# Network one's turns and attentions in two stages without inner barriers, and query tiles in the order 128, 256, 512, 384 keys

## The chip, the cores and the metric

The program runs on one core of a Trainium2 chip, in one launch. The metric is the device time of the whole program in microseconds (us). The engines are TensorE (PE, matrix products), VectorE (DVE), ScalarE (ACT), GpSimd (POOL) and SyncE (SP), which issues the weight loads.

## The reference

Two networks of two layers each, on 512 tokens of width 1024, in float32. Network one, per layer: rmsnorm, one wide projection, and three mixers side by side, then an output projection and a squared-relu feed-forward. The mixers are

- `mla_attention`: 8 heads, queries and keys of 96 (64 plain, 32 with rope), values of 64, causal softmax;
- `dsa_attention`: 4 heads of 64 with one shared key and value head; a query sees only the 128 keys that an index score ranks highest (`lax.top_k`), found here as a mask;
- `retention`: 4 heads of 64, `(q k^T * decay) v`, written in the kernel without chunks, then a group norm times `silu(gate)`.

Network two, per layer: a gated delta rule, a block-compressed attention with 6 heads, two further softmax attentions of 6 heads each over the same tokens, a stick-breaking attention, and a gated feed-forward with a convolution. Of it the change touches only the two softmax attentions ("nsa", 12 heads in one call).

## The kernel before

Tokens are tiled by 128, so a head has four query tiles; causal tile t has (t+1) x 128 keys. A stage (`Core.stage`, L151) is one block of instruction streams, one per engine, written out by hand; at its end all engines meet in a barrier (its instructions are at L168). With `goes_on=True` a stage ends without a barrier and the next one's instructions follow in the same streams; then the waits must be written out. `stay_busy` (L178) issues eight transposes without use on PE at a stage's end.

Network one's mixers are five stages in a row in each layer:

1. "mlaT" (`transpose_tiles`, L463): 16 jobs, the turns of 8 key heads and then 8 query heads. A job is four 128-column transposes into PSUM bank i % 8; even jobs are kept (copied to SBUF) by ACT, odd ones by DVE.
2. "mla" (`softmax_attention`, L2570): 32 units, a unit being a head and a query tile. For unit i PE issues the scores of i (L2611, float32, two passes), then the turn of the probabilities of i-2 (L2625), then the values of i-4 (L2635). DVE adds the causal mask (L2653), takes the maximum (L2654); ACT takes the exponential with the row sum (L2686) and then copies the turned probabilities of unit i-2 (L2697). The turn of unit u waits for the exponential of u and the copy of u-2. After a head's last tile DVE divides (L2667, L2669). GpSimd ropes the other mixers' columns meanwhile.
3. "mixT" (`transpose_tiles`): seven jobs, the shared "dsa" key (split in a high and a low part, by ACT and then DVE, L535), two of its queries, two of the retention's queries, two of its keys. ACT first does the Silu of the gate (L4086) and two casts.
4. "ret" (`retention`, L2700): PE's dots (L2720) for pairs of heads in banks 0 to 5, the product with the decay on DVE (L2751), the outputs (L2730) in banks 6 and 7, squares and copies on ACT. DVE also finishes the search of the largest index scores (L1126, L1128, L1130), makes the first query's low part (L459) and sums the squares (L2761). GpSimd multiplies the gate (L2766).
5. "dsa" (`softmax_attention`): 16 units; scores as two single-pass products and the mask as a third (L2614), so DVE adds no mask. GpSimd does the retention's group norm.

In the attentions the units of a head run in the order of 128, 256, 384 and 512 keys. "nsa" of network two is the same function with a `guest`, the tail of the compressed attention, whose steps are placed by unit number; it already follows its turns without a barrier.

Of the kernel before, what the change touches and what calls it, by code (L numbers as in the profile page):

```python
# [462 lines left out]
def transpose_tiles(c, name, jobs, also_pool=None, also_act=None, first_dve=None, wait_source=None, by_dve=None):  # L463
# [15 lines left out]
    with c.stage(name, "turned", "act_kept", "dve_kept", "made") as (block, turned, act_kept, dve_kept, made):  # L479
# [4 lines left out]

        @block.tensor
        def _(pe):
            def wait_kept(i):
                if i in by_dve:
                    pe.wait_ge(dve_kept, by_dve.index(i) + 1)
                else:  # L490
                    pe.wait_ge(act_kept, by_act.index(i) + 1)

            for i, (src, m, dst, scale) in enumerate(jobs):
                if i >= 8:
                    wait_kept(i - 8)
# [12 lines left out]
            if len(jobs) >= 8:  # L508
                wait_kept(len(jobs) - 8)
            c.stay_busy(pe, len(jobs) % 8, 8)  # L510

        @block.scalar
        def _(act):
            if also_act is not None:
                also_act(act)
            for i, (src, m, dst, scale) in enumerate(jobs):
                if i in by_act:
                    act.wait_ge(turned, i + 1)
                    if i in split:
# [4 lines left out]
                    ins.then_inc(act_kept, 1)  # L524

        @block.vector
        def _(dve):
            if first_dve is not None:
                first_dve(dve, made)
            for i, (src, m, dst, scale) in enumerate(jobs):  # L530
# [6 lines left out]
                if i in by_dve:  # L537
# [3 lines left out]
                    ins.then_inc(dve_kept, 1)  # L541

# [590 lines left out]
SEARCH_EARLY = 15  # L1133

# [1435 lines left out]
def softmax_attention(c, name, heads, meanwhile=None, beside=None, ready=None, guest=None):  # L2570
# [7 lines left out]
    units = [(h, t) for h in range(len(heads)) for t in range(TT)]  # L2578
    U = len(units)
    with ExitStack() as ctx:  # L2580
# [8 lines left out]
        with c.stage(name, "scores", "maxed", "probs", "turned", "probsT", "outs", "kept", "step", "pool_step",  # L2589
# [8 lines left out]
            def _(pe):  # L2598
                for i in range(U + 4):
                    if i < U:  # L2600
# [6 lines left out]
                        if t == 0 and ready is not None:  # L2607
                            ready(pe, beside_done, h)
# [9 lines left out]
                    if 0 <= u < U:  # L2618
# [3 lines left out]
                        elif guest is not None:  # L2622
                            guest.wait_turn(pe)
                        for j in range(units[u][1] + 1):
# [4 lines left out]
                    if 0 <= u < U:  # L2629
                        h, t = units[u]  # L2630
                        pe.wait_ge(probsT, u + 1)
                        if t == 0 and h >= 2:
                            pe.wait_ge(kept, h - 1)
                        for j in range(t + 1):
# [9 lines left out]
            def _(dve):  # L2644
                step = Steps(dve, step_sem)
                for i in range(U + 5):
# [14 lines left out]
                    if 0 <= u < U and units[u][1] == TT - 1:  # L2661
# [14 lines left out]
            def _(act):  # L2676
                for i in range(U + 3):
                    if i < U:
# [5 lines left out]
                        if t == 0 and h >= 4:  # L2684
# [15 lines left out]
def retention(c, name, qT, kT, v, decay, out, gate, g_ret, var, beside, queries):  # L2700
# [5 lines left out]
    with ExitStack() as ctx:  # L2706
        sb = lambda n, s: ctx.enter_context(c.tile(name + n, s, F32))
        inner = sb("inner", [P, RET_H, TT, SEQ])
        sq, warm = sb("sq", [P, RET_H, TT, HD]), sb("warm", [P, 1])
        with c.stage(name, "dots", "inners", "outs", "kept", "step", "squares", "q_his", "q_los") as (  # L2710
                block, dots, inners, outs, kept, step_sem, squares, q_his, q_los):
            @block.tensor
            def _(pe):
                def dot_pairs(k):
                    pair, j = k // TT, k % TT
                    if k >= 3:
                        pe.wait_ge(inners, 2 * (k - 2))
                    for b in range(2):
                        r = slice(HD * b, HD * (b + 1))
                        nc.tensor.matmul(c.ps[:, 2 * (k % 3) + b, 0:SEQ - j * P],  # L2720
                                         kT[r, pair, j * P:(j + 1) * P], qT[r, pair, j * P:SEQ],
                                         start=True, stop=True).then_inc(dots, 1)

                def out_of(h):
                    pe.wait_ge(inners, 2 * TT * (h // 2 + 1))
                    if h >= 2:
                        pe.wait_ge(kept, h - 1)
                    for t in range(TT):
                        for j in range(t + 1):
                            ins = nc.tensor.matmul(  # L2730
                                c.ps[:, 6 + h % 2, t * HD:(t + 1) * HD],
                                inner[:, h, j, (t - j) * P:(t - j + 1) * P],
                                v[:, j, h * HD:(h + 1) * HD], start=(j == 0), stop=(j == t))
                    ins.then_inc(outs, 1)

                for k in range(6):
                    dot_pairs(k)
                out_of(0)
                for k in range(6, 2 * TT):
                    dot_pairs(k)  # L2740
                for h in range(1, RET_H):
                    out_of(h)
                c.stay_busy(pe, 0, 8)

            @block.vector
            def _(dve):
                step = Steps(dve, step_sem)
                for i in range(RET_H * TT):
                    pair, j, b = i // (2 * TT), i // 2 % TT, i % 2
                    dve.wait_ge(dots, i + 1)  # L2750
                    nc.vector.tensor_tensor(inner[:, 2 * pair + b, j, 0:SEQ - j * P],  # L2751
# [1655 lines left out]
```

## Time and profile before

| | us |
|---|---|
| median of 3 runs | 3170.96 (3170.54 to 3171.04) |
| the profiled execution | 3171.36 |
| its span, first to last instruction | 3169.3 |

| engine | busy us | share |
|---|---|---|
| PE | 3076.0 | 97% |
| DVE | 1810.4 | 57% |
| ACT | 1288.5 | 41% |
| POOL | 402.4 | 13% |

The shares are means over stages that have different limits. The ends of PE's instructions are modelled, and one can begin while the one before it still runs, so PE's stalls are read from starts. In the rows a time is from the span's start.

### The profile page before, as it was taken

What the parts mean: (1) busy time and instruction counts of PE and PEld (TensorE: products, weight loads), DVE (VectorE), ACT (ScalarE), POOL (GpSimd) and SP (SyncE); (2) the same over time, 40 slices, a digit from 0 to 9 for tenths busy, and PEclk for the clock granted to TensorE, in tenths of its full rate; (3) what the DMA queues carried; (4) which work ended last, traced back from release to release, by engine and by line L of the source; (5) the groups of instructions that cost most, each with busy time, mean ns of one, the idle gap of its engine ahead of it and who ended that gap; (6) DMA issues with size and microseconds to landing.
All of it is one profiled execution on the core that took longest, in us unless ns stands there. A gap on an engine that the chain in (4) does not pass through costs nothing. (4 is left out here: it accounts for less than half of the span.)

```text
span 3169.3 us, 48184 instructions
## 1 busy us (share of the span) xinstructions
PE 3076.0 (97%) x19220; PEld 2618.1 (83%) x19220; DVE 1810.4 (57%) x3220; ACT 1288.5 (41%) x2673; POOL 402.4 (13%) x398
## 2 busy tenths in 40 slices
PE   8999999999999999999999999999999999999997
PEld 6878888888878888888888888888888878888886
DVE  4876443435965434357566467474575665574655
ACT  4445432334354423244374343232643643332325
POOL 1031000001031000002213302010003034010010
PEclk9999999999999999999999999999999999999999
DMA  4110222222201322322100122223222000222221
GB/s 176 57 54 28 94 93 98 102 84 89 83 2 54 107 93 94 125 74 100 67 1 2 42 80 100 90 93 117 81 101 80 1 2 22 94 97 95 91 95 63
DMA packets 37293, 239.38 MB, mean 76 GB/s; under 512 B 4432, under 2 KB 5200, under 8 KB 15056
## 3 DMA queue, kind: packets, MB, share of 16 engines
q1 hardware_dynamic: 36080, 233.58, 21.6%
q8 instruction: 154, 2.52, 0.3%
q10 hardware_dynamic: 992, 2.73, 0.3%
q14 instruction: 67, 0.55, 0.1%
HBM read 234.19 MB, written 2.10 MB: 75 GB/s over the span
## 5 line engine op out<-in xcount | busy, mean ns | idle before, releaser
L278 PE MATMUL ps<-b_hl,bff_whl 128*128 128x512 f32 (+1 forms) x840 | 313.6, 373 | 0.0
L279 PE MATMUL ps<-b_hl,bff_whl 128*128 128x512 f32 (+1 forms) x840 | 313.2, 373 | 0.0
L280 PE MATMUL ps<-b_hl,bff_whl 128*128 128x512 f32 (+1 forms) x840 | 313.2, 373 | 0.0
L261 DVE SCALAR_TENSOR_TENSOR bff_whl<-ring,b_cols,bff_whl 128x512 fp32r<-128x512 f32 (+3 forms) x288 | 194.7, 737 | 186.4 <-ACT bff_whl L248 186.1
L248 ACT ACTIVATE bff_whl<-ring,b_cols 128x512 fp32r<-128x512 f32 (+3 forms) x288 | 173.4, 674 | 168.7 <-PE ps L280 168.7
L278 PE MATMUL ps<-a_hl,aff_whl 128*128 128x512 f32 (+1 forms) x648 | 238.9, 369 | 0.0
L279 PE MATMUL ps<-a_hl,aff_whl 128*128 128x512 f32 (+1 forms) x648 | 238.5, 368 | 0.0
L280 PE MATMUL ps<-a_hl,aff_whl 128*128 128x512 f32 (+1 forms) x648 | 238.5, 368 | 0.0
L258 DVE TENSOR_TENSOR aff_whl<-ring,aff_whl 128x512 fp32r<-128x512 f32 x160 | 99.8, 686 | 216.6 <-ACT aff_whl L246 216.5
L278 PE MATMUL ps<-aff_whl,a_hl 128*128 128x512 f32 (+5 forms) x544 | 204.9, 377 | 4.5 <-DVE a_hl L680 2.2
L279 PE MATMUL ps<-aff_whl,a_hl 128*128 128x512 f32 (+5 forms) x544 | 202.3, 372 | 0.0
L280 PE MATMUL ps<-aff_whl,a_hl 128*128 128x512 f32 (+5 forms) x544 | 202.3, 372 | 0.0
L278 PE MATMUL ps<-aff_whl,a_u 128*128 128x512 f32 x512 | 199.5, 390 | 0.0
L261 DVE SCALAR_TENSOR_TENSOR aff_whl<-ring,a_gains,aff_whl 128x512 fp32r<-128x512 f32 (+3 forms) x192 | 131.9, 748 | 117.9 <-ACT aff_whl L248 117.5
L280 PE MATMUL ps<-aff_whl,a_u 128*128 128x512 f32 x512 | 199.2, 389 | 0.0
L279 PE MATMUL ps<-aff_whl,a_u 128*128 128x512 f32 x512 | 199.2, 389 | 0.0
L246 ACT CAST aff_whl<-ring 128x512 fp32r<-128x512 f32 x160 | 87.5, 621 | 268.4 <-PE ps L280 263.6
L248 ACT ACTIVATE aff_whl<-ring,a_gains 128x512 fp32r<-128x512 f32 (+3 forms) x192 | 120.0, 697 | 174.9 <-PE ps L280 174.9
L280 PEld LDWEIGHTS ps<-b_hl,bff_whl 128*128 128x128 f32 x840 | 158.2, 188 | 27.9
L279 PEld LDWEIGHTS ps<-b_hl,bff_whl 128*128 128x128 f32 x840 | 158.2, 188 | 27.7
L278 PEld LDWEIGHTS ps<-b_hl,bff_whl 128*128 128x128 f32 x840 | 158.2, 188 | 27.6
L258 DVE TENSOR_TENSOR bff_whl<-ring,bff_whl 128x512 fp32r<-128x512 f32 x128 | 84.6, 720 | 141.7 <-ACT bff_whl L246 141.6
(512 smaller groups left out, 7240.7 us busy)
## 6 DMA issues: line engine op xcount, KB each, us to landing
ring<-in_a_w_ff SPq DMA_DIRECT2D x64, 1024.0 KB, 4.7
ring<-in_b_w_up SPq DMA_DIRECT2D x32, 1024.0 KB, 4.8
ring<-in_a_w_in SPq DMA_DIRECT2D x16, 1024.0 KB, 4.8
ring<-in_b_w_down SPq DMA_DIRECT2D x16, 1024.0 KB, 4.8
ring<-in_b_w_in_att SPq DMA_DIRECT2D x12, 1024.0 KB, 4.7
ring<-in_b_w_up SPq DMA_DIRECT2D x16, 768.0 KB, 4.1
ring<-in_b_w_in_conv SPq DMA_DIRECT2D x12, 768.0 KB, 4.2
ring<-in_a_w_out SPq DMA_DIRECT2D x8, 1024.0 KB, 4.9
```

Source lines behind the costliest of these rows:

```text
L246: self.c.nc.scalar.copy(self.part(j, 0, k), src[:, k, :]).then_inc(self.hi_made, 1)
L248: self.c.nc.scalar.activation(self.part(j, 0, k), src[:, k, :], ACT.Copy, scale=g[:, row + k:row + k + 1]).then_inc(self.hi_made, 1)
L258: self.c.nc.vector.tensor_tensor(self.part(j, 1, k), src[:, k, :], self.part(j, 0, k).bitcast(F32), ALU.subtract).then_inc(self.lo_made, 1)
L261: self.c.nc.vector.scalar_tensor_tensor(out=self.part(j, 1, k), in0=src[:, k, :], scalar=g[:, row + k:row + k + 1], in1=self.part(j, 0, k) ...
L278: nc.tensor.matmul(bank, sh, mh, start=start, stop=False)
L279: nc.tensor.matmul(bank, sh, ml, start=False, stop=False)
L280: return nc.tensor.matmul(bank, sl, mh, start=False, stop=stop)
```

## The change

"mlaT" and "mla" become one stage, and "mixT", "ret" and "dsa" another: `transpose_tiles` and `retention` are called with `goes_on=True`, issue no transposes without use, and return the waits that the next part needs. The jobs of "mlaT" alternate, key and query of a head after each other. Those of "mixT" begin with the retention's, and the Silu and the two casts move from ACT's first place to its last. The retention's tiles are allocated with the others of the stage. In `softmax_attention` the tiles of a head run in the order (0, 1, 3, 2), for all three attentions of both networks.

```diff
+TILE_ORDER = (0, 1, 3, 2)
-    units = [(h, t) for h in range(len(heads)) for t in range(TT)]
+    units = [(h, t) for h in range(len(heads)) for t in TILE_ORDER]
...
+class TurnsInFront:
+    def __init__(self, kept):
+        self.kept = kept
+    def wait_score(self, pe, i):
+        h, t = i // TT, i % TT
+        if t == 0 and h < MLA_H:
+            self.kept(pe, 2 * h)
+            self.kept(pe, 2 * h + 1)
+        if i < 4:
+            self.kept(pe, 8 + i)
+    def wait_turn(self, pe, u):
+        self.kept(pe, 12 + u)
+    def wait_out(self, pe, h):
+        self.kept(pe, 14 + h)
+class RetentionInFront:
+    def wait_score(self, pe, i):
+        if i == 0:
+            self.turned(pe, 4)
+            self.turned(pe, 5)
+            pe.wait_ge(self.cleared, 1)
+            pe.wait_ge(self.q_los, 1)
+    def wait_turn(self, pe, u):
+        pe.wait_ge(self.outs_kept, u + 1)
+    def wait_out(self, pe, h):
+        pe.wait_ge(self.outs_kept, RET_H - 1 + h)
+    def wait_norm(self, pool):
+        pool.wait_ge(self.gated, 1)
+        pool.wait_ge(self.outs_kept, RET_H)
+        pool.wait_ge(self.sums, RET_H)
...
 transpose_tiles:
-            if len(jobs) >= 8:
-                wait_kept(len(jobs) - 8)
-            c.stay_busy(pe, len(jobs) % 8, 8)
+            if not goes_on:
+                if len(jobs) >= 8:
+                    kept(pe, len(jobs) - 8)
+                c.stay_busy(pe, len(jobs) % 8, 8)
...
 retention, PE:
                 if k >= 3:
                     pe.wait_ge(inners, 2 * (k - 2))
+                else:
+                    kept_turn(pe, 2 * k)
+                    kept_turn(pe, 2 * k + 1)
...
                 if h >= 2:
                     pe.wait_ge(kept, h - 1)
+                elif h == 0:
+                    kept_turn(pe, 6)
...
-            c.stay_busy(pe, 0, 8)
 retention, POOL and ACT:
+            pool.wait_ge(made, 1)
+            pool.wait_ge(acted, 1)
...
+                kept_turn(act, 5)
+                kept_turn(act, 6)
...
 first_layer:
-            jobs = [(lambda t, h=h: kcat[:, t, h, :], MLA_QK, kT[0:MLA_QK, h, :], 1.0) for h in range(MLA_H)]
-            jobs += [(lambda t, h=h: q4[:, t, h, :], MLA_QK, qT[0:MLA_QK, h, :], mla_scale) for h in range(MLA_H)]
-            transpose_tiles(c, "mlaT", jobs)
+            jobs = []
+            for h in range(MLA_H):
+                jobs += [(lambda t, h=h: kcat[:, t, h, :], MLA_QK, kT[0:MLA_QK, h, :], 1.0),
+                         (lambda t, h=h: q4[:, t, h, :], MLA_QK, qT[0:MLA_QK, h, :], mla_scale)]
+            kept, all_turned, _, _ = transpose_tiles(c, "mlaT", jobs, goes_on=True)
...
-            jobs = [(lambda t: (proj[:, t, A_AK:A_AK + DSA_D],) * 2, P, SplitKeys(kbhi[:], kblo), 1.0)]
+            jobs = []
+            for i in range(2):
+                jobs += [(tile_of(A_RQ + i * P), P, rqT[:, i, :], RET_D ** -0.5),
+                         (tile_of(A_RK + i * P), P, rkT[:, i, :], 1.0)]
+            jobs += [(lambda t: (proj[:, t, A_AK:A_AK + DSA_D],) * 2, P, SplitKeys(kbhi[:], kblo), 1.0)]
             jobs += [(tile_of(A_AQ + i * P), P, qbT[:, i, :], DSA_D ** -0.5) for i in range(2)]
-            jobs += [(tile_of(A_RQ + i * P), P, rqT[:, i, :], RET_D ** -0.5) for i in range(2)]
-            jobs += [(tile_of(A_RK + i * P), P, rkT[:, i, :], 1.0) for i in range(2)]
...
-            transpose_tiles(c, "mixT", jobs, clear, gates)
+            kept, _, made, acted = transpose_tiles(c, "mixT", jobs, clear, last_act=gates, goes_on=True)
...
+            def query_low(dve, done, i):
+                if i in (0, 4, 8):
+                    dve.wait_ge(front.q_his, i // 4 + 2)
+                    queries.low(dve, done, i // 4 + 1)
```

## Rows read from the trace of the kernel before

**Rows 1.** Page, busy us, share of the span and instructions of each engine

```profile
PE 3076.0 (97%) x19220; PEld 2618.1 (83%) x19220; DVE 1810.4 (57%) x3220; ACT 1288.5 (41%) x2673; POOL 402.4 (13%) x398
```

**Rows 2.** Stretches: length, busy of PE, PEld, DVE, ACT, POOL; granted clock; DMA

```profile
201.60:250.97 49.37, 46.96 (x312) 36.60 (x312) 32.23 (x83) 29.17 (x96) 24.73 (x18) 1.00 0.00 1
...
257.80:261.90 4.10, 4.06 (x16) 2.66 (x16) 2.35 (x5) 3.84 (x6) 2.78 (x4) 0.58 0.01 2
...
941.32:944.72 3.40, 2.70 (x16) 1.52 (x16) 2.23 (x5) 3.31 (x6) 2.78 (x4) 1.00 0.00 0
```

**Rows 3.** Timeline, "mlaT" to "mla": start, us, engine, line, count [idle before <-releaser]

```profile
200.32 1.04 PE L180 MATMUL ps<-const_a 128*128 128x128 f32 x8
200.52 0.69 DVE L540 TENSOR_SCALAR a_qT<-ps 96x512 f32<-96x512 f32 x1 [0.19 <-PE ps L504]
...
202.15 0.30 DVE L2653 TENSOR_TENSOR ps<-ps,const_a 128x128 f32<-128x128 f32 x1 [0.94 <-PE ps L2611]
...
206.79 0.41 PE L2625 MATMUL ps<-const_a,mlap 128*128 128x128 f32 x2 [0.38 <-ACT mlapT L2697]
```

**Rows 4.** Timeline, one head of "mla" and the next one's 512 score

```profile
226.49 0.56 DVE L2654 TENSOR_REDUCE mlanegmax<-ps 128x1 f32<-128x384 f32 x1
226.69 1.08 PE L2611 MATMUL ps<-a_kT,a_qT 96*128 96x512 f32 x2
227.08 0.58 ACT L2686 ACTIVATE mlap<-ps,mlanegmax 128x384 f32<-128x384 f32 x1 [0.68 <-DVE mlanegmax L2654]
...
227.60 0.39 PE L2625 MATMUL ps<-const_a,mlap 128*128 128x128 f32 x2
...
228.13 0.69 DVE L2654 TENSOR_REDUCE mlanegmax<-ps 128x1 f32<-128x512 f32 x1
...
228.86 0.69 ACT L2686 ACTIVATE mlap<-ps,mlanegmax 128x512 f32<-128x512 f32 x1 [0.95 <-DVE mlanegmax L2654]
...
229.44 0.65 PE L2611 MATMUL ps<-a_kT,a_qT 96*128 96x256 f32 x2
...
230.04 0.63 PE L2625 MATMUL ps<-const_a,mlap 128*128 128x128 f32 x4
...
232.33 1.08 PE L2611 MATMUL ps<-a_kT,a_qT 96*128 96x512 f32 x2
```

**Rows 5.** Timeline, the end of "mla"

```profile
246.98 0.63 PE L2625 MATMUL ps<-const_a,mlap 128*128 128x128 f32 x4 [0.72 <-ACT mlapT L2697]
...
248.09 0.59 ACT L2697 COPY mlapT<-ps 128x512 f32<-128x512 f32 x1 [0.88 <-PE ps L2635]
```

**Rows 6.** Timeline, "mixT", "ret" and the start of "dsa"; last row: layer two

```profile
251.01 1.09 PE L506 MATMUL ps<-const_a,a_proj 128*64 128x128 f32 x16 [0.30 <-PEq L168]
...
252.04 2.84 PE L504 MATMUL ps<-const_a,a_proj 128*128 128x128 f32 x24
...
256.84 0.68 DVE L540 TENSOR_SCALAR a_rkT<-ps 128x512 f32<-128x512 f32 x1
...
257.84 5.84 PE L2720 MATMUL ps<-a_rqT,a_rkT 64*128 64x512 f32 x24 [2.09 <-PEq L168]
...
259.55 3.36 DVE L2751 TENSOR_TENSOR retinner<-ps,const_a 128x512 f32<-128x512 f32 x8 [2.03 <-PE ps L2720]
...
263.61 2.44 PE L2730 MATMUL ps<-a_proj,retinner 128*128 128x64 f32 x20
...
266.71 1.15 DVE L2751 TENSOR_TENSOR retinner<-ps,const_a 128x256 f32<-128x256 f32 x4 [1.44 <-PE ps L2720]
...
273.42 1.40 DVE L2761 TENSOR_REDUCE a_var<-retsq 128x4 f32<-128x256 f32 x4
...
275.68 0.29 DVE L2654 TENSOR_REDUCE dsanegmax<-ps 128x1 f32<-128x128 f32 x1 [0.86 <-PE ps L2614]
...
942.49 0.69 DVE L2751 TENSOR_TENSOR retinner<-ps,const_a 128x512 f32<-128x512 f32 x1 [1.45 <-PE ps L2720]
```

**Rows 7.** Waits of PE in "nsa", 1568.75 to 1642.6: us in total, times, longest

```profile
PE ps L2625 <- ACT nsapT L2697: 4.1, 5, 2.3
```

More of the change, by code:

```diff
@@ L478, in transpose_tiles @@
     split = [i for i, job in enumerate(jobs) if isinstance(job[2], SplitKeys)]
-    with c.stage(name, "turned", "act_kept", "dve_kept", "made") as (block, turned, act_kept, dve_kept, made):
+    with c.stage(name, "turned", "act_kept", "dve_kept", "made", "acted", goes_on=goes_on) as (
+            block, turned, act_kept, dve_kept, made, acted):
         if also_pool is not None:
@@ L524, in _ @@
                     ins.then_inc(act_kept, 1)
+            if last_act is not None:
+                last_act(act, acted)
         @block.vector
@@ L2606, in _ @@
                             guest.wait_score(pe, i)
-                        if t == 0 and ready is not None:
+                        if front is not None:
+                            front.wait_score(pe, i)
+                        if i % TT == 0 and ready is not None:
                             ready(pe, beside_done, h)
@@ L2660, in _ @@
                     u = i - 5
-                    if 0 <= u < U and units[u][1] == TT - 1:
+                    if 0 <= u < U and u % TT == TT - 1:
                         h = units[u][0]
@@ L2697, in _, with retention @@
                         nc.scalar.copy(pT[:, u % 2, 0:nk], c.ps[:, 4 + u % 2, 0:nk]).then_inc(probsT, 1)
-def retention(c, name, qT, kT, v, decay, out, gate, g_ret, var, beside, queries):
+def retention(c, name, qT, kT, v, decay, out, gate, g_ret, var, beside, queries,
+              tiles, kept_turn, made, acted):
     nc = c.nc
[L2706 to L2742, printed above, removed]
-                c.stay_busy(pe, 0, 8)
[L2745 to L2751, printed above, removed]
-                                            c.ps[:, 2 * (i // 2 % 3) + b, 0:SEQ - j * P],
-                                            decay[:, 2 * pair + b, 0:SEQ - j * P], ALU.mult).then_inc(inners, 1)
-                for i in range(9):
-                    beside(dve, step, i)
-                if queries is not None:
-                    dve.wait_ge(q_his, 1)
-                    queries.low(dve, q_los, 0)
-                for h in range(RET_H):
-                    dve.wait_ge(squares, h + 1)
-                    nc.vector.tensor_reduce(var[:, :, h], sq[:, h], AX.X, ALU.add)
-            @block.gpsimd
-            def _(pool):
-                for t in range(TT):
-                    nc.gpsimd.tensor_tensor(gate[:, t], gate[:, t], g_ret, ALU.mult)
-            @block.scalar
-            def _(act):
-                nc.scalar.activation(warm[:], decay[:, 0, 0:1], ACT.Exp)
-                if queries is not None:
-                    for f in range(queries.n):
-                        queries.high(act, f).then_inc(q_his, 1)
-                for h in range(RET_H):
-                    act.wait_ge(outs, h + 1)
-                    o = c.ps[:, 6 + h % 2, 0:TT * HD].rearrange("p (t d) -> p t d", t=TT)
-                    nc.scalar.activation(sq[:, h], o, ACT.Square).then_inc(squares, 1)
-                    nc.scalar.copy(out[:, :, h, :], o).then_inc(kept, 1)
@@ L2781, in group_norm @@
+    return kept, q_his, q_los, sums, gated
 def group_norm(nc, pool, step, out, gate, sums, half):
```

122 lines of the change are left out of this document (101 added, 21 removed).

## The prediction

> **What bounds the kernel now.** I read the engines' shares first: TensorE (PE) is busy 97% of the span [rows 1]; its busy ends are modelled, so the share hides short stalls. So I read start against start in the timeline. The stages that the change touches were found with the table by stretch; it shows the attention stage "mla" with PE working in 46.96 of 49.37 us, VectorE (DVE) in 32.23, ScalarE (ACT) in 29.17 [rows 2]. Inside it PE's instructions follow one another without a hole: one head (four query tiles) takes 232.33 - 226.69 = 5.64 us of PE start to start [rows 4]. The time that isn't PE's own work lies at the seams of stages (fill, barrier, drain), and once a head. The retention stage is different: there PE waits for DVE.
>
> The change acts in both layers of network one (joins, order) and both of network two (order alone). Layer two of network one repeats layer one 683.52 us later (the stretches 257.80 and 941.32 begin the same stage).
>
> **Join of the turns and "mla".** Before, the last transposes end where PE's eight filler transposes begin, 200.32; they and the barrier hold the first mask addition on DVE until 202.15 [rows 3]. Afterwards PE can issue the first score at 200.32, but DVE still has the keep of turn 15 to finish, 200.52 + 0.69 = 201.21 [rows 3]. So DVE, and with it the first exponential and turn, starts at about 201.24, 0.91 us earlier: not the 1.33 by which PE is freed, since DVE is late next. The turn at 206.79 waited a further 0.38 us for a copy [rows 3]. That wait goes: with 512 keys third, the fourth unit's scores are shorter and its chain starts earlier, while the third's is 0.24 us longer (maximum and exponential of 512 for 384, [rows 4]); I take 0.3. Added waits: two semaphores a head on PE, both signalled one or more turns earlier, behind them only PE's own queue; I cost them at nothing since PE is bound by the array here; if each cost 0.05 us uncovered, 8 heads x 2 x 2 layers would be 1.6 us. Other ends of this term: 0 if DVE's queue eats it, 1.6 if the third unit costs nothing. Taken: 1.2 a layer, **2.4 us**. GpSimd's ropes start after the last turn, about 1 us earlier, and nobody waits for them.
>
> **Order of the tiles, steady state.** PE does score(i), turn(i-2), values(i-4). The turn of a 512 tile waits for maximum, exponential and one copy. Before, from PE's end of issue of the 512 scores (227.60) to the turn (230.04) passed 2.44 us, after which PE waits for ACT [rows 4]. The PE work between is about 2.32: a 512 score takes 227.60 - 226.69 = 0.91 in two passes, one of 256 should take 0.48, and 230.04 - 229.44 is 0.60 [rows 4]. So a stall of some 0.12 a head is hidden where no idle shows. In the new order the turn of 512 comes after a 384 score and 384 values more: PE work between about 2.8, needed 2.44, no stall. The tight one is then 384: the PE work from its score to its turn is 2.32 less a block of values twice over (values of 384 for 512, -0.22) plus a transpose (+0.11), about 2.2; needed is 2.44 less the difference in maximum (0.69 to 0.56) and exponential (0.69 to 0.58), 2.20 [rows 4]. The slack is nil, within 0.1 either way. I take the gain of 0.12 for the seven heads after the first: 0.85 a layer, **1.7 us**; bounds -1.6 (a new stall of 0.1 each) to +1.9. ACT pairs exponential and copy more evenly, which buys nothing while PE is the bound. In "dsa" and network two's "nsa" the mask is a product on PE and DVE has one step less, so there is no such stall to win in their steady state, and 0.3 us more slack for the 384 turn.
>
> **Order, drain.** At the end of "mla" the turn of the last 512 tile waits 0.72 us, and its copy at 248.09 holds the last values [rows 5]. With 384 last, maximum, exponential and copy are 0.13, 0.11 and 0.10 shorter, and the copy of 512 lies before, under PE's values. Of the 0.72 about 0.1 goes. PE's last values then stand behind a 0.59 copy that ACT, idle for 0.88, could begin only when PE had finished another tile's values [rows 5]; I estimate 0.4 of it uncovered, and nearly all of that goes. I take 0.5 a stage; six stages ("mla", "dsa", "nsa", two layers each): **3.0 us**, bounds 1 and 4.
>
> **"nsa", the rest.** Five turns wait 4.1 us for a copy, one of them 2.3 [rows 7]; the largest is in the fill, where the third unit is now 512 and some 0.25 us later, and the periodic ones wait for a copy that is now of 384 (0.1 shorter) with PE arriving slightly later. +0.5 less 0.25 a layer: **0.5 us**, bounds -2 and +3, since DVE's and ACT's guest work is placed by unit number and meets other sizes.
>
> **Second join: turns, retention, "dsa".** This is the largest term. Before: PE ends the seven jobs at 251.01 + 1.03 + 24 x 0.11 = 254.7 [rows 6]. ACT first did Silu and two casts, so DVE's five keeps end at 256.84 + 0.68 = 257.52, and only after the barrier come the dots (257.84) and the first product with the decay, 259.55 [rows 6]. Afterwards: the retention's four jobs first, Silu last. PE turns rq, rk pairs by 251.01 + 16 x 0.11 = 252.8, the shared key by 253.8; ACT casts it by about 254.6; DVE then has three passes of 0.69 (two subtractions, one keep) to 256.75. Dots 0 and 1 are issued at 254.7, behind the transposes, so the first decay product starts at about 256.8: 2.75 earlier than 259.55, and 2.15 earlier than 942.49 in layer two (258.97 in layer one's time) [rows 6].
>
> DVE then runs its eight products in the same 3.36; the next dots wait for DVE's products as before, then PE does 20 value passes in 2.44 (before they began at 263.61), and the products before 266.71 come out at about 264.05, 2.66 earlier in layer one and 2.0 in layer two [rows 6]. From there to the end of the variance sums (273.42 + 1.40 = 274.82) DVE's chain is unchanged, so it ends 272.16. The third barrier goes: the first maximum of "dsa" came at 275.68, 0.86 after that sum [rows 6]; PE issues those scores behind its last retention values, and DVE takes the maximum at once. Together 2.66 + 0.86 = 3.5 and 2.0 + 0.86 = 2.9, 6.4 us. Silu and the second table load, now late on ACT, end near 260, before ACT's next customer (retention's first output, about 263.3); if ACT were late there, PE would wait at the third output, not before. GpSimd's gate product moves after Silu, and its norm starts when the sums are there; the stage ends 20 us later, so both are hidden.
>
> What PE's clock takes off: PE stood idle 2.09 us before 257.84 [rows 6], and in 257.80 to 261.90 the granted clock was 0.58, that is mostly 1.2 GHz, while the same dots in layer two (941.32 to 944.72) ran at 1.00, 2.4 GHz [rows 2]. After the change the filler transposes are gone and PE waits for DVE's products in three gaps of 0.6 to 0.8 us between 256.4 and 259.3. If the clock falls there, dots 4 and 5 and the 20 value passes (2.44) run at half speed: up to 1.5 us a layer is lost. One layer in two: -0.8. Bounds 3 and 7; taken **5.6 us**.
>
> The Trainium skill, "TensorE: Matmul & The Clock Gate", "What's actually happening", says that an array that has been too little busy is passed only half its clock and gets the rest back after a stretch of activity. By that rule the lost filler speaks against the change, and both layers would lose; that is part of rival B.
>
> **Sum.** 2.4 + 1.7 + 3.0 + 0.5 + 5.6 = 13.2 us. The profiled execution took 3171.36 (span 3169.3), 0.4 over the median of 3170.96. 3171.36 - 13.2 = 3158.2, as a median 3157.8.
>
> **Rivals.**
> (A) The joins give, the order doesn't: PE is the bound in all three attentions, the 0.12 isn't a stall and the drains are as long. For it: no idle shows in steady state; against it: the 0.72 before the last turn. Then 0.9 x 2 + 5.6 = 7.4, 3163.6.
> (B) The retention chain keeps its end: the dots wait for DVE twice more, PE's clock falls in both layers, and only about half of the 6.4 arrives. For it: the 0.58 of rows 2; against it: DVE's own passes are unchanged in length. 13.2 - 2.4 = 10.8, 3160.2.
> (C) Slower: in the new order the turn of the 384 tile waits for the copy of the 256 tile behind its exponential. Its slack in "mla" is nil by the numbers above; there are 12 heads in each layer of network one and 12 in each of network two, 48 in all. Without the order's 5.2 the joins give 8.0, so it decides from 8.0 / 48 = 0.17 us a head; at 0.35 it costs 16.8 and the time is 3179.8. Against it: in 32 of those heads DVE has no mask addition and the slack is about 0.3.
> (D) The change doesn't do what it says: the first stage's scores still wait, since DVE's keeps and the last turn end together; the seams give only barrier times (0.3 us of PE at each of six). Then 1.8 + 3.0, 3166.2.
> (E) More than forecast: "nsa" gains at each periodic stall and no clock falls: 3153.
>
> **Chances.** Forecast (3155.5 to 3160) 0.55, A 0.13, B 0.13, C 0.04, D 0.04, E 0.11. A measurement of this kernel can tell about 0.2%, 6.3 us. Above 3164.6 lie D and the upper part of A: no change 0.09; slower than 3177.3 only C, 0.04; faster 0.87. The range takes in E, B and most of A: 3152.5 to 3164.
>
> **What would show it.** Right: no filler transposes between turns and scores; the first mask addition of "mla" right behind DVE's last keep; a head in "mla" of 5.50 to 5.55 us instead of 5.64; the first decay product about 5.8 us after the second join starts; the first "dsa" maximum right behind the variance sums; a shorter wait before the last turn in all six attentions. Wrong: PE idle before the 384 turns in every head; granted clock below 1 from about 6 us after the join's start in both layers; decay products that begin where they did; a longer fill in "nsa".

## The result, and the profile after

| | us | runs |
|---|---|---|
| before | 3171.0 (3170.54 to 3172.64) | 4 |
| after | 3152.25 (3149.84 to 3155.82) | 4 |
| after / before | 0.9942 [0.9931, 0.9954] | |

The change makes the kernel faster by 18.7 us, where 13.2 were forecast. The median lies under the forecast's 3155.5 to 3160 and 0.25 us under the lower end of the whole range, 3152.5 to 3164. The profiled execution of the changed kernel took 3151.79, its span is 3150.0, that is 19.3 less than before. How much of that is the change's own is settled further below, where the same kernel is run again.

The page after, engines (busy us, share, instructions), against [rows 1]. PE's work is 14.6 us less in sum, part of it the 48 transposes without use that are gone and part the clock.

```profile
PE 3061.4 (97%) x19172; PEld 2605.8 (83%) x19172; DVE 1808.8 (57%) x3220; ACT 1292.5 (41%) x2673; POOL 402.1 (13%) x398
```

The stages, from PE's first instruction of one to that of the next, in the table by stretch (columns as in [rows 2]). Kernel before: "mlaT" and "mla"; "mixT" to "dsa" of layer one and of layer two; "nsa" with its turns; the delta rule and what follows up to the second "nsa"; the last 599 us; and one stretch inside the delta rule of the first network-two layer.

```profile
193.32:251.01 57.69, 55.00 (x384) 44.43 (x385) 37.72 (x91) 33.96 (x105) 24.77 (x19) 1.00 0.00 1
251.01:299.13 48.12, 44.57 (x344) 39.04 (x345) 29.87 (x65) 25.69 (x70) 11.50 (x10) 0.96 0.01 2
...
934.57:982.03 47.46, 43.20 (x345) 37.91 (x346) 29.80 (x65) 25.66 (x71) 11.47 (x10) 1.00 0.00 1
1544.70:1642.69 97.99, 90.91 (x804) 86.74 (x805) 59.80 (x146) 59.82 (x173) 5.03 (x5) 0.97 0.07 23
...
1685.78:2428.97 743.19, 733.21 (x5076) 631.27 (x5077) 448.48 (x702) 274.77 (x517) 126.68 (x124) 1.00 0.24 81
...
2570.04:3169.28 599.24, 573.20 (x4296) 491.49 (x4296) 347.72 (x540) 210.57 (x402) 97.41 (x103) 0.99 0.22 74
...
1715.70:1719.10 3.40, 3.04 (x56) 3.04 (x58) 0.00 (x0) 0.91 (x3) 0.31 (x1) 0.50 0.00 0
```

The same stages of the kernel after:

```profile
192.50:247.89 55.39, 52.79 (x376) 43.55 (x377) 37.93 (x91) 34.08 (x104) 24.78 (x19) 1.00 0.00 1
247.89:291.81 43.92, 41.20 (x328) 35.91 (x329) 28.50 (x65) 26.46 (x70) 11.49 (x10) 1.00 0.01 1
924.89:968.81 43.92, 41.19 (x328) 35.91 (x329) 28.49 (x65) 26.46 (x70) 11.50 (x10) 1.00 0.01 1
1531.50:1628.25 96.75, 90.61 (x804) 86.26 (x805) 59.95 (x146) 60.87 (x173) 5.02 (x5) 0.96 0.07 23
1671.33:2412.44 741.11, 730.90 (x5076) 628.79 (x5077) 448.77 (x702) 274.78 (x517) 126.70 (x124) 1.00 0.24 81
...
2552.19:3150.00 597.81, 572.26 (x4296) 490.53 (x4296) 347.62 (x540) 210.68 (x402) 97.34 (x103) 0.99 0.22 74
```

Per stage: "mla" 57.69 to 55.39, -2.30; layer two shows the same (57.69 to 55.37). "mixT" to "dsa" 48.12 to 43.92, -4.20, and 47.46 to 43.92, -3.54; the two layers differed before by 0.66 because the granted clock fell in layer one [rows 2], and don't after. "nsa" 97.99 to 96.75, -1.24 (layer two -1.36). The feed-forwards are unchanged. The last two pairs are code that the change doesn't touch: -2.08 and -1.43. There the clock differs: the stretch from 1715.70 ran at half clock before (0.50) and its counterpart after didn't. That isn't all of it, as the second profile of the same kernel shows further below. The sum is 2.30 + 2.32 + 4.20 + 3.54 + 1.24 + 1.36 + 3.51 = 18.5, and with 0.8 in the first 193 us, untouched too, 19.3.

The first join in the timeline after, against [rows 3]. The stage starts at 192.50 (before 193.32).

```profile
199.70 0.69 DVE L548 TENSOR_SCALAR a_qT<-ps 96x512 f32<-96x512 f32 x1 [0.19 <-PE ps L509]
...
200.31 0.28 DVE L2717 TENSOR_TENSOR ps<-ps,const_a 128x128 f32<-128x128 f32 x1
...
203.62 0.63 PE L2687 MATMUL ps<-const_a,mlap 128*128 128x128 f32 x4 [0.73 <-ACT mlapT L2761]
```

DVE goes from the last keep to the first mask addition without idle time, 7.81 us after the stage's start; before it was 202.15 - 193.32 = 8.83. But the turn of the 512 tile, now the third unit's, waits 0.73 us in the fill. Before, two turns shared that wait: the fourth unit's, of 512 keys, waited 0.38 [rows 3], and the third's, of 384 keys, 0.29:

```profile
205.24 0.52 PE L2625 MATMUL ps<-const_a,mlap 128*128 128x128 f32 x3 [0.29 <-ACT mlapT L2697]
```

One head of "mla" after, and its end, against [rows 4, 5]:

```profile
224.77 0.86 PE L2671 MATMUL ps<-a_kT,a_qT 96*128 96x384 f32 x2
...
227.19 0.65 PE L2671 MATMUL ps<-a_kT,a_qT 96*128 96x256 f32 x2
...
227.68 0.51 PE L2687 MATMUL ps<-const_a,mlap 128*128 128x128 f32 x3
...
230.29 0.86 PE L2671 MATMUL ps<-a_kT,a_qT 96*128 96x384 f32 x2
...
244.24 0.52 PE L2687 MATMUL ps<-const_a,mlap 128*128 128x128 f32 x3 [0.59 <-ACT mlapT L2761]
244.59 2.12 PE L2699 MATMUL ps<-a_proj,mlapT 128*128 128x64 f32 x18
245.24 0.48 ACT L2761 COPY mlapT<-ps 128x384 f32<-128x384 f32 x1 [0.66 <-PE ps L2699]
```

A head takes 230.29 - 224.77 = 5.52 us instead of 5.64. The difference lies in one place. From the start of the 256 tile's scores to the start of the turn behind them it is 227.68 - 227.19 = 0.49 us; before it was 230.04 - 229.44 = 0.60 [rows 4], where that turn was the 512 tile's. This is the hidden stall of the prediction. At the end the last turn waits 0.59 instead of 0.72, and the 18 value products (4, 8 and 6, for 256, 512 and 384 keys) run through without a break while ACT copies.

The second join, against [rows 6]:

```profile
247.89 1.28 PE L509 MATMUL ps<-const_a,a_proj 128*128 128x128 f32 x10 [0.30 <-PEq L168]
...
253.64 3.28 DVE L2818 TENSOR_TENSOR a_ret_inner<-ps,const_a 128x512 f32<-128x512 f32 x8
...
253.76 0.70 PE L2786 MATMUL ps<-a_rqT,a_rkT 64*128 64x256 f32 x4 [0.18 <-DVE a_qbT L548]
...
254.99 0.49 PE L2786 MATMUL ps<-a_rqT,a_rkT 64*128 64x128 f32 x4 [0.53 <-DVE a_ret_inner L2818]
...
255.91 1.77 PE L2786 MATMUL ps<-a_rqT,a_rkT 64*128 64x512 f32 x8 [0.44 <-DVE a_ret_inner L2818]
...
267.43 1.40 DVE L2828 TENSOR_REDUCE a_var<-a_ret_sq 128x4 f32<-128x256 f32 x4
...
268.75 0.28 DVE L2718 TENSOR_REDUCE dsanegmax<-ps 128x1 f32<-128x128 f32 x1
```

The decay products start 5.75 us after the stage's start (before 259.55 - 251.01 = 8.54), the variance sums 19.54 after it (before 22.41), and the first maximum of "dsa" follows them without idle time, 20.86 after (before 24.67).

### The profile page after: what moved, and what is told of

The parts are those of the page before. It is cut to its first block and busy times, and to the rows that moved or that the text cites. A ratio compares the mean times of both kernels' runs of the same rounds, so it can differ in the third digit from the quotient of the medians.

```text
span 3150.0 us, 48082 instructions
## 1 busy us (share of the span) xinstructions
PE 3061.4 (97%) x19172; PEld 2605.8 (83%) x19172; DVE 1808.8 (57%) x3220; ACT 1292.5 (41%) x2673; POOL 402.1 (13%) x398
```

## The experiments

All kernels were timed beside the kernel before on the same chip; a ratio is to that one. The kernel before spread over 3165.65 to 3173.37 in 21 runs of the first group, so the ratios alone don't separate effects of 1 us. The lengths of the stages that the change touches do: in network one they agree to 0.1 us between kernels that are equal there, in "nsa" to 0.2 where it runs equally long at half clock.

### e1: the joins alone

```diff
 (after)
-TILE_ORDER = (0, 1, 3, 2)
+TILE_ORDER = (0, 1, 2, 3)
```

> The changed kernel with the tiles of a head back in the order 128, 256, 384, 512; both joins stay. Theory (the order gives in all three attentions): a head of mla takes 5.64 us of PE start to start again (5.52 in the changed kernel), the last turn of mla waits about 0.88 again, mlaT to the end of mla is about 56.5 us (55.4 changed, 57.7 before), mixT to the end of dsa about 43.8 (43.45 changed), nsa with its turns 97.7 (96.4 changed); total 3157 to 3160. Rival A (the joins give, the order does not): mla's stretch stays at 55.4 and nsa's at 96.4, total like the changed kernel's 3152. Theory on the rest: about 3.5 us of the changed kernel's gain are three stretches of half clock in network two, outside the change, that its profile no longer shows; whether they are in this run decides 3.5 us of its time either way.

3161.35 in 6 runs, 0.9971 [0.996, 0.9983]. "mla", "mixT" to "dsa", and "nsa" of this kernel:

```profile
192.97:249.58 56.61, 53.89 (x376) 43.53 (x377) 37.58 (x91) 33.91 (x104) 24.77 (x19) 1.00 0.00 1
249.58:293.73 44.15, 41.47 (x329) 36.02 (x329) 28.60 (x65) 26.22 (x70) 11.49 (x10) 1.00 0.01 1
1534.91:1631.56 96.65, 89.51 (x805) 85.12 (x805) 59.72 (x147) 59.96 (x173) 5.01 (x5) 0.98 0.07 23
```

The first join is worth 57.69 - 56.61 = 1.08 a layer, the second 47.46 - 44.15 = 3.31. Two heads take 236.54 - 225.25 = 11.29 us (starts of the 512 scores), 5.64 each, as before. The last turn waits 0.72, as before; the 0.88 of the expectation is the wait of ACT's copy [rows 5]. "nsa" is 96.65 and not 97.7 because only 3.4 us of it ran at half clock in this layer; in the other, with 6.8, it is 97.97.

### e2: the order alone

```diff
 (before)
+TILE_ORDER = (0, 1, 3, 2)
-    units = [(h, t) for h in range(len(heads)) for t in range(TT)]
+    units = [(h, t) for h in range(len(heads)) for t in TILE_ORDER]
...
-                        if t == 0 and ready is not None:
+                        if i % TT == 0 and ready is not None:
...
```

The last lines stand for four like ones: a head's first and last tile are now told by the unit's number.

> The kernel before with the new order of tiles alone, no join. Theory: a head of mla 5.52 us, its last turn waits about 0.75 instead of 0.88, nsa with its turns 96.4 instead of 97.7, dsa 0.4 shorter; the gains per layer about 1.2 (mla), 0.4 (dsa), 1.3 (nsa), together 5.8 us: 3165, less up to 3.5 if stretches of half clock in network two go. Rival (384 turns stall, or order neutral): heads of 5.64 or more and 3171.

3164.52 in 10 runs, 0.9981 [0.9972, 0.999]. "mla", "mixT" to "dsa", and "nsa":

```profile
193.41:249.86 56.45, 53.81 (x385) 44.44 (x385) 37.98 (x91) 34.12 (x105) 24.77 (x19) 1.00 0.00 1
249.86:296.97 47.11, 42.63 (x344) 37.92 (x345) 29.80 (x65) 25.92 (x70) 11.51 (x10) 1.00 0.01 2
1540.94:1637.59 96.65, 90.46 (x805) 86.51 (x805) 59.94 (x147) 60.86 (x173) 5.02 (x5) 0.96 0.07 23
```

The order is worth 1.24 in "mla", 0.35 in "dsa", 1.34 in "nsa" (97.99 to 96.65, both with 6.8 us at half clock). With the joins' 1.08 the 2.32 of "mla" comes out, and 3.31 + 0.35 is 3.66 where the whole change shows 3.54: the parts add up.

### e3, e4: what in the second join pays, Silu's place, the jobs' order or the barriers

```diff
 (e3, from after: ACT does Silu and the casts before its keeps again)
-            if also_act is not None:
-                also_act(act)
+            if last_act is not None:
+                last_act(act, acted)
...
-            if last_act is not None:
-                last_act(act, acted)
 (e4, from before, with the tile order: the jobs' new order in "mlaT" and "mixT",
  also_act behind ACT's keeps; barriers and transposes without use stay)
```

> The changed kernel with the gate's Silu and the two casts again ahead of ACT's keeps in the joined stage; joins and job order stay. Theory (the second join pays because the retention's keeps come first on ACT and DVE): Silu with its table load holds ACT until about 2.7 us after the stage's start, so the keep of the first retention query comes at +2.8 instead of +0.7, the dots at +3.8 as before the edit, but the key's cast and DVE's three passes behind it later by about 1 us: first decay product at about +6.8 instead of +5.8, total +1 to +2 us. Rival (only the barriers count, ACT's order does not): +5.8 and no difference.

> The kernel before with the new order of tiles, the new order of the turn jobs and Silu last, but with all barriers and filler transposes kept. Theory: the jobs' order buys nothing behind a barrier beyond the end of DVE's keeps (from +6.55 to about +5.8 us of the stage), so retention's first product comes at about +7.8 (layer one; +8.6 before, +5.8 changed) and mixT to the end of dsa takes about 46 (47.6 and 47.0 before, 43.45 changed); total 3163 less up to 3.5 for half clock elsewhere. Rival: the job order is the whole gain of the second join and the barriers are free: +5.8 or so and 43.5.

Silu first: 3154.97 in 4 runs, 0.9949 [0.9934, 0.9964]; the stage is 44.49 in both layers against 43.92, so its place is worth 0.57 a layer. The first product came 6.32 us after the stage's start, where 6.8 were expected and the changed kernel has 5.75. The jobs' order and Silu's new place without the joins: 3166.42 in 10 runs, 0.9988 [0.9979, 0.9998], no better than the tile order alone, and the stage got longer where about 46 us were expected. Its two layers:

```profile
248.93:297.86 48.93, 43.98 (x344) 38.54 (x345) 30.02 (x65) 26.34 (x70) 11.49 (x10) 0.97 0.01 2
932.04:981.82 49.78, 45.30 (x344) 39.48 (x345) 30.06 (x65) 26.36 (x70) 11.51 (x10) 0.93 0.00 1
```

And its timeline where the retention's dots begin:

```profile
256.60 3.96 PE L2721 MATMUL ps<-a_rqT,a_rkT 64*128 64x512 f32 x16 [2.81 <-PEq L168]
...
258.68 2.27 DVE L2752 TENSOR_TENSOR retinner<-ps,const_a 128x512 f32<-128x512 f32 x4 [4.03 <-PE ps L2721]
```

With a barrier behind it, Silu at the end is what all engines wait for: PE idles 2.81 us, then has half its clock, and the products start 9.75 us after the stage's start, 1.2 later than in the kernel before and 2 later than expected. Only without the barrier does work that nobody waits for cost nothing at the end of ACT's list. With the barriers gone and Silu still first (e3), 47.46 - 0.35 - 44.49 = 2.6 us of the gain are there. How these 2.6 divide between the barriers and the jobs' order no run shows.

### e5: is DVE the bound of the second join

```diff
 (after)
-            kept, _, made, acted = transpose_tiles(c, "mixT", jobs, clear, last_act=gates, goes_on=True)
+            kept, _, made, acted = transpose_tiles(c, "mixT", jobs, clear, by_dve=(1, 3), last_act=gates, goes_on=True)
...
                     kept_turn(pe, 2 * k + 1)
+                    if k == 2:
+                        pe.wait_ge(inners, 1)
```

> The changed kernel with one pass less on DVE before the retention: the sixth turn job of mixT (dsa queries) is kept by ACT instead of DVE, and dots 2 wait for DVE's first product, which stands behind its reading of the key's bank. Theory (after the join DVE's three passes of 0.69 set when the first decay product starts): it starts at +5.1 us of the stage instead of +5.8, everything behind moves with it, mixT to the end of dsa 43.2 instead of 43.9 in each layer, 1.4 us in all. Rival (PE's dots, ready at about +5.1, or ACT are the bound by then): no change, or a loss where ACT's later Silu and table load hold up the first output.

Both query keeps go to ACT. 3153.86 in 4 runs, 0.9946 [0.9931, 0.9961], no different in time from the change itself; but the stage is 43.27 (43.24 in layer two) against 43.92, and the first product begins right behind the key's low parts, 5.08 us after the stage's start at 247.99:

```profile
251.62 1.39 DVE L543 TENSOR_TENSOR a_kblo<-ps,a_kbhi 64x512 fp32r<-64x512 f32 x2 [0.96 <-ACT a_kbhi L526]
...
253.07 3.28 DVE L2820 TENSOR_TENSOR a_ret_inner<-ps,const_a 128x512 f32<-128x512 f32 x8
```

One DVE pass of 0.69 out of the chain shortens the stage by 0.65: DVE's passes were the chain, as the prediction had it.

### e6, e7, e10: the drain, and the stall in the middle of "mla"

```diff
 (e6, after)
-    units = [(h, t) for h in range(len(heads)) for t in TILE_ORDER]
+    units = [(h, t) for h in range(len(heads)) for t in (TILE_ORDER if h < len(heads) - 1 else LAST_ORDER)]
+LAST_ORDER = (1, 3, 2, 0)
 (e7, after; the two passes that centre the retention's values)
-                elif i in (10, 12):
-                    t = slice(i - 10, i - 8)
+                elif i in (9, 13):
+                    t = slice((i - 9) // 2, (i - 9) // 2 + 2)
```

> The changed kernel with the last head of each attention in the order 256, 512, 384, 128. Theory (at the end of an attention PE waits for the chain maximum, exponential, copy of the last tile, so its size sets the wait): the last wait of a turn falls from 0.75 (mla) and 0.42 (dsa, nsa) to 0.2 or less; 0.5, 0.4 and 0.4 us a stage, 2.6 in all. Rival (the wait is set by the copy before, whose tile is now larger): the wait stays, or the turn of 384 in the last head stalls.

> The changed kernel with the two long DVE passes that centre the retention's values (1.4 us each) after the maxima of units 9 and 13 (tiles of 256) instead of 10 and 12 (512 and 128). Theory (behind the 512 tile they meet the 384 turn, which has no slack, and cost the 0.86 us stall that the changed kernel shows there, 0.57 before): the stall falls to 0.1 to 0.2 us, mlaT to the end of mla 54.7 instead of 55.4 in each layer. Rival (any place costs the same, since DVE is full there): 55.4 or more.

A last head that ends with its 128 tile: 3150.26 in 4 runs, 0.9936 [0.9921, 0.995]; "mla" 54.86 against 55.39, "mixT" to "dsa" 43.76 against 43.92, "nsa" 95.3 against 95.4 at an equal clock. The drain still held 0.5 us in "mla", as expected; in "dsa" it held 0.16 and in "nsa" 0.1, where 0.4 each were expected.

Moving the passes one unit earlier and one later gave nothing: 3153.81 in 4 runs, 0.9946 [0.9931, 0.9961], "mla" 55.44. The stall of 0.70 at 216.63, before a turn of 384, went, and one of 0.68 came, at the 512 tile's turn before it:

```profile
215.47 0.63 PE L2687 MATMUL ps<-const_a,mlap 128*128 128x128 f32 x4 [0.68 <-ACT mlapT L2761]
```

The theory that each pass is tight only where it stands fell. The new one: DVE is in arrears from the summing pass of unit 8 on, and what matters is how much more it is given before it has caught up; the second pass, at unit 13, was free.

```diff
 (e10, after)
-                elif i in (10, 12):
-                    t = slice(i - 10, i - 8)
+                elif i in (13, 17):
+                    t = slice((i - 13) // 2, (i - 13) // 2 + 2)
```

> The changed kernel with the two centring passes after units 13 and 17, so that neither follows the 1.2 us sum at unit 8 closely. In the run with units 9 and 13 the first met DVE's arrears from that sum and the second cost nothing. Theory (what counts is DVE's arrears, not the tile): no stall of 0.8 us in the third or fourth head, mlaT to the end of mla 54.6 in each layer, 1.5 to 1.7 us in all. Rival (a long pass always stalls a turn once): 55.4.

3149.46 in 4 runs (3147.38 to 3155.86), 0.9935 [0.9922, 0.9949]; "mla" is 54.51, 0.88 shorter a layer, and no turn waits there. But the passes themselves also got shorter. First the four passes of the changed kernel (ns, least, median, most), then those of this one and GpSimd's operation beside the first of them:

```profile
L4133 DVE SCALAR_TENSOR_TENSOR a_proj<-a_vsum,a_proj x4: 1539/1608/1651, 213.2 to 893.0; 128x512 f32<-128x512 f32 x4
```

```profile
L4133 DVE SCALAR_TENSOR_TENSOR a_proj<-a_vsum,a_proj x4: 679/680/683, 216.8 to 898.5; 128x512 f32<-128x512 f32 x4
...
216.97 1.65 POOL L2562 TENSOR_TENSOR a_kcat<-a_proj,const_a 128x512 f32<-128x512 f32 x1
```

So this experiment alone doesn't tell the two causes apart: later passes, or passes of 0.68 for 1.6. e7 helps: its second pass stood behind unit 13 too, took 1.55 us there (217.47), and no turn waited. At that place a long pass costs nothing, so later passes are enough. Whether passes of 0.68 in the old places would have ended the stall as well was not tried.

### e8: the half clock of "nsa"

```diff
 (after)
+                    if guest is not None and u == 2:
+                        c.stay_busy(pe, 7, 20)
```

> The changed kernel with 20 filler transposes on PE in the fill of nsa, in front of the third turn, where PE waits 3 us. Theory (PE's clock falls after that wait, whatever the kernel, and each such stretch costs nsa 1.3 us): the profile shows one stretch of half clock less in each nsa, turns and nsa take 95.4 instead of 96.7, 2.6 us in all, and the scatter of the runs shrinks. Rival (DVE's guest work is the bound in that fill, the slow clock is hidden under it): the stretches go and the time stays; or the filler, 2.2 us, ends after the wait and costs up to 0.5 us.

20 transposes without use stand before the third turn. 3150.94 in 4 runs, 0.994 [0.9923, 0.9957]. "nsa" of both layers, against 96.75 and 96.62:

```profile
1530.99:1625.06 94.07, 90.12 (x824) 85.70 (x825) 59.95 (x146) 60.57 (x173) 5.01 (x5) 1.00 0.07 24
2412.46:2507.88 95.42, 91.47 (x824) 87.36 (x825) 60.05 (x147) 60.45 (x173) 5.02 (x5) 0.98 0.07 24
```

Over the profiles this stage's length goes with the time that it spends at half clock. With the new order it is 94.1 us at none (only with the transposes), 95.4 to 95.5 at 3.4 us, and 96.6 to 96.8 at 6.8 us. In e10's profile, where nothing in this stage was edited, it is 98.7 at 13.7 us, in both layers; that execution was the slowest of e10's four:

```profile
1529.98:1628.67 98.69, 93.14 (x804) 89.00 (x805) 60.00 (x147) 60.80 (x173) 5.02 (x5) 0.93 0.07 23
```

With the old order it is 96.7 at 3.4 us (e1) and 98.0 at 6.8 us (before). So at an equal time at half clock the new order is worth 1.2 to 1.3 a layer, and 3.4 us at half clock cost 1.3 us of time, 1.0 beyond 6.8 us. In the changed kernel PE waits 2.9 us for the third turn, in the fill, and the 6.8 us from 1560.30 run at half clock. The waits of PE in that stage (us, times, longest), the stretch, and a turn of the timeline; then a turn of the kernel before:

```profile
PE ps L2687 <- ACT nsapT L2761: 3.5, 4, 2.9
...
1560.30:1567.10 6.80, 6.16 (x29) 5.88 (x30) 3.98 (x12) 4.58 (x14) 0.00 (x0) 0.50 0.01 2
...
1574.81 0.41 PE L2687 MATMUL ps<-const_b,b_kv2T 128*128 128x128 f32 x2 [0.21 <-ACT nsapT L2761]
```

```profile
1587.95 0.41 PE L2625 MATMUL ps<-const_b,b_kv2T 128*128 128x128 f32 x2 [0.52 <-ACT nsapT L2697]
```

The place of these stretches shows what the transposes do. In the eleven profiles without them, 22 stages, a stretch at half clock begins 28.5 to 31.5 us after the stage's start every time, around the third turn (29.4 us after it in the changed kernel). In the four stages with them (e8, e11) none begins there; the 10 us from 1556.00 of e8 have a granted clock of 1.00. What is left in e8's second layer and in both of e11 begins 19.8 to 21.0 us after the start, ahead of the transposes, and 13 of the 22 have such an early stretch too. By the stage's length the transposes are worth 1.3 us a layer (95.4 to 94.1), which the total of 4 runs can't show.

### e9, e11: the same kernel again, and four edits together

> The changed kernel itself once more, nothing edited. Theory (where PE's half clock falls is a matter of each execution, and the first profile of the changed kernel was a lucky one in network two): stages outside network two's nsa and delta rule repeat to 0.1 us; nsa takes 95.4 or 96.7, the stretch from deltaT on 741.2 to 744 us in the first layer and 597 to 600 in the second, by the number of half-clock stretches in them; the median over more runs comes out near 3154 instead of 3152.25, 16 to 17 us under the kernel before. Rival (the change itself keeps the clock up there): no half clock after deltaT again, and 3152.

> The changed kernel with ACT's keep of the sixth job, the last head in the order 256, 512, 384, 128, the centring passes after units 13 and 17, and the 20 fillers in nsa's fill. If they add: mla 54.1 (-0.53 last head, -0.8 centring), mixT to the end of dsa 43.1 (-0.65, -0.17), nsa with its turns 94 or 95.3 by its half clock; per layer about 2.1 in network one and 1.4 in network two, 7 us in all: about 3147. Rival (they meet in the same slack and give less): 3150.

The unedited kernel after: 3154.43 in 5 runs (3153.95 to 3156.49), 0.9949 [0.9935, 0.9962], 2.2 us more than at first. The stretches of network two in its profile, and the stage of the delta rule inside the first:

```profile
1670.62:2412.81 742.19, 731.20 (x5076) 628.94 (x5077) 448.32 (x701) 274.70 (x517) 126.64 (x124) 1.00 0.24 81
2552.62:3152.61 599.99, 574.78 (x4296) 493.36 (x4296) 347.30 (x540) 210.51 (x402) 97.17 (x103) 0.98 0.22 74
...
1677.22:1752.39 75.17, 70.10 (x1776) 66.83 (x1777) 49.67 (x103) 26.90 (x78) 40.50 (x52) 1.00 0.01 3
```

Network one's stages are as in its first profile to 0.05 us; network two's untouched code takes 1.1 and 2.2 us more than there, 742.19 + 599.99 = 1342.2, which is what the kernel before took (1342.4). The 2.2 go with two stretches at half clock in the second layer, from 2583.5 and 2634.7, which the first profile doesn't have. The 1.1 don't: that stage of the delta rule takes 75.17 us here and 74.05 there, at a granted clock of 1.00 in both, and why stays open. Over the 13 profiles this untouched code takes 1338.7 to 1342.4 us, with the kernel before at the upper end. So of the 19.3 us between the first two profiles, 3.5 in the rest of network two and 0.8 at the start belong to the two executions and not to the change. What is left is 2.31 x 2 + 4.20 + 3.54 + 1.3 x 2 = 15.0 us, of which 0.66 are the half clock of layer one's retention, which fell in none of the profiles with the join. All nine runs of the changed kernel together have a median of 3154.4, 16.6 under 3171.0 and inside the range of the prediction, though still under 3155.5.

The edits of e5, e6, e8 and e10 in one kernel: 3147.86 in 5 runs (3145.55 to 3150.11), 0.9927 [0.9915, 0.9939], the fastest of all; "mla" and "mixT" to "dsa":

```profile
192.76:246.77 54.01, 52.60 (x377) 43.73 (x377) 36.47 (x91) 34.30 (x104) 24.87 (x19) 1.00 0.01 1
246.77:289.84 43.07, 41.00 (x329) 35.93 (x329) 27.79 (x64) 27.07 (x71) 11.48 (x10) 1.00 0.01 2
```

0.88 + 0.53 is 1.41 and the first stage is 1.38 shorter; 0.65 + 0.16 is 0.81, and the second is 0.85 shorter. Its interval and that of the unedited kernel on the same chip (0.9935 to 0.9962) overlap a little; 2.2 us a layer shorter stages in network one, 4.5 in all, are the surer evidence. "nsa" came out longer than expected in one layer, 96.4 (expected 94 or 95.3), with 6.8 us at half clock from 1547.2, ahead of the transposes; the other layer is 95.3.

## Why the prediction was right in its steps, and where its sizes were off

The forecast's mechanism came: both joins pay, and so does the order. Its size was nearer rival E, and E's two conditions are both met: "nsa" gained at its periodic stalls, and no clock fell in the retention. By its steps:

- **Join of the turns and "mla"**, 1.2 a layer: 1.08 measured. DVE was late next, as said: in its stage the mask addition came 1.02 earlier, forecast 0.91. The further 0.3 for the wait in the fill [rows 3] didn't come. The fourth unit's 0.38 did go, and the third's 0.29 with it, but the third unit is now the 512 tile and its own turn waits 0.73. It was also booked in the wrong term: e1, with the joins and the old order, still has the 0.29 and the 0.38.
- **Order, steady state**, 0.12 a head: 5.64 became 5.52, and the 0.12 went from before the 512 tile's turn, as said. The 384 turn, for which no slack was found, doesn't wait in the steady heads. Rival C fell there.
- **Drain of "mla"**: with the steady state 1.35 was forecast for the order, 1.24 measured. The copy went under PE's values as said. What was missed lies in the middle of the stage, which had not been read: the passes that centre the retention's values hold one turn, of 384 keys, for 0.70 us, where before they held one of 512 for 0.53.
- **Drain of "dsa"**: 0.5 forecast, 0.35 measured.
- **"nsa"**: the term that was too small, 0.75 a layer forecast with its drain, 1.3 measured. The fill kept its sum: the first turn's wait went from 1.10 to 0.55, the third's from 2.32 to 2.85. But the waits beyond the third turn's, 4.1 - 2.3 = 1.8 [rows 7], fell to 3.5 - 2.9 = 0.6. The prediction took 0.1 off each for the shorter copy; three periodic ones of 0.31 to 0.53 became two of 0.21, and the last turn's is about 0.2 for 0.4. That PE reaches the turn with more of its own work done was counted as "slightly later".
- **Second join**: first maximum of "dsa" forecast 3.5 and 2.9 earlier, measured 3.81 in layer one (24.67 to 20.86) and 3.15 in layer two (24.01 to 20.86). The first decay product was forecast at 5.8 and came at 5.75. Of the 0.3 too little, 0.2 lie between there and the sums (22.41 to 19.54, 2.87 for 2.66 forecast), 0.1 at the last barrier (from the sums' start to the maximum 2.26 became 1.32). That DVE's passes are the chain is shown by e5.
- **PE's clock in the retention**: 0.8 was taken off for a fall in one layer of two, and this was wrong. PE's three gaps are 0.18, 0.53 and 0.44 us, not 0.6 to 0.8, and the stage's granted clock is 1.00 in both layers. Rival B fell. What went was 2.09 us of idle time before the dots [rows 6]; e4 lengthened it to 2.81, and there the granted clock of the stage was 0.97 and 0.93. Over all profiles, three of the six stages with 2.09 or 2.81 us of idle time there (kernel before, e2, e4) have a stretch at half clock, and none of the 20 without it. The Trainium skill, "TensorE: Matmul & The Clock Gate", "What's actually happening", says that the clock is set by how busy PE has been recently. These rows agree with that, but they don't show it alone, since barriers, idle time and transposes went together. The prediction applied the rule to the transposes that go and not to the idle time that goes with them.

Rival A is excluded by e2's ratio and D by e1's. The sum without the clock's deduction was 14.0 us, with what layer one's half clock had cost counted as gained; the like sum of the stages is 15.0. The terms missed it in both directions: "nsa" gave 2.6 for 1.5 and the second join 7.0 for 6.4, but "mla" 4.6 for 5.1 and "dsa" 0.7 for 1.0. So the mechanism was right, and that the sum came so near is in part the luck of misses that offset each other. The first measurement's 18.7 has 2 to 4 us in it that come from the unchanged stages and differ from execution to execution.

## What to carry to other kernels

A barrier costs more than its own time: it makes every engine wait for work that nobody needs yet, so moving work that nobody needs yet to the end pays only once the barrier is gone. Here the stage takes 47.1 us with the barriers and the old order of jobs (e2), 48.9 and 49.8 with the barriers and the new one, in part at half clock (e4), and 43.9 without the barriers. In a pipeline bound by one engine, put the longest unit where the most work of the bound engine follows it, and look for the seams, not at the steady state alone. Where stages are unchanged but their times differ, compare the granted clock before crediting the edit, and profile the same kernel twice: 1.1 us here came at an equal clock.

## What was not expected of the hardware

The same program's executions differ by 8 us (3165.65 to 3173.37 over 21 runs of the kernel before). In the two profiles of the changed kernel 2.2 us lie in stretches at half clock that come in one execution and not in the other, on identical code, and 1.1 us in a stage that runs at full clock in both. In "nsa" 3.4 us at half clock cost 1.0 to 1.3 us. Twenty transposes without use in the wait of 2.9 us kept the clock up behind that wait in four stages of four, where it fell in 22 of 22 without them, and did nothing about the stretches that begin 8 us or more before it.

A DVE pass with two operands in SBUF took 0.68 us in one place and 1.6 in another beside the same GpSimd work. Where DVE's pass began while GpSimd's operation ran (213.16 and 212.90 in the changed kernel), DVE took 1.56 and that operation stayed at 1.27, but GpSimd's next one, from 214.25, took 1.60. Where DVE began first (216.8, before 216.97), it took 0.68 and GpSimd's took 1.65. The Trainium skill, "SBUF — State Buffer", "Who interferes with whom", says that a DVE instruction with two inputs in SBUF contends with a GpSimd one that reads SBUF, for a pair of ports that whoever issues first holds while the other blocks; the trace agrees, with 0.4 us lost by GpSimd when DVE is first, and 0.9 by DVE and 0.3 by GpSimd's next operation when GpSimd is first.
